# A hybrid streaming encoder step on one core: the running streams' attention in 128x32 tiles of the array

## The reference

```
k = concat([k_cache, k_new], 1); v = concat([v_cache, v_new], 1)      # 528 rows
sc = einsum('bqhd,bkhd->bhqk', q, k).astype(f32) * d**-0.5
sc = sc + rel_bias            # group A;  group B: unselected keys get -inf
p = softmax(sc); o = einsum('bhqk,bkhd->bqhd', p, v)
```

## Time and profile before

| | us |
|---|---|
| device time, median of 3 runs (2888.13 to 2890.64) | 2889.68 |
| span of the profiled execution | 2886.9 |
| TensorE busy: matmuls / weight loads | 2714.9 (94%) / 2441.3 (85%) |
| VectorE / ScalarE / GpSimd busy | 1381.5 / 673.3 / 155.3 |

### The profile page before, as it was taken

One profiled execution on the slowest core, in us unless ns is written; L12 is line 12 of the kernel. 1 busy time (PEld: TensorE's weight loads), 2 busy tenths in 40 slices (PEclk: granted clock), 3 DMA queues, 4 the chain that ended last, 5 costly groups with the idle time before them and its releaser, 6 DMA issues. The chain is left out here.

```text
span 2886.9 us, 38111 instructions
## 1 busy us (share of the span) xinstructions
PE 2714.9 (94%) x15412; PEld 2441.3 (85%) x15412; DVE 1381.5 (48%) x2539; ACT 673.3 (23%) x1228; POOL 155.3 (5%) x116
## 2 busy tenths in 40 slices
PE   6999999999998999976988989989799999999998
PEld 6999999999997799975777766667799999999997
DVE  5333333333335598986777723333333333333335
ACT  4101111111022323133666532221211111111112
POOL 0000000000001021831000000000000000000000
PEclk9999999999998999998999989999899999999999
DMA  4111111111003121213000335540211111111101
GB/s 150 54 44 44 44 44 44 44 33 39 22 17 107 48 94 63 79 48 119 30 23 30 110 104 178 178 161 1 88 44 44 44 44 44 44 44 44 44 7 66
DMA packets 117273, 180.97 MB, mean 63 GB/s; under 512 B 11424, under 2 KB 75048, under 8 KB 117168
## 3 DMA queue, kind: packets, MB, share of 16 engines
q1 hardware_dynamic: 113520, 165.35, 17.3%
q0 software_dynamic: 3648, 14.16, 1.4%
HBM read 155.73 MB, written 31.11 MB: 65 GB/s over the span
## 5 line engine op out<-in xcount | busy, mean ns | idle before, releaser
L347 DVE TENSOR_TENSOR f_silu<-f_silu,f_pgu 128x384 f32<-128x384 f32 x132 | 73.2, 554 | 802.2 <-ACT f_silu L287 802.2
L185 PE MATMUL f_pgu<-r_T_hi,f_gh 128*128 128x384 f32 x1056 | 359.7, 341 | 15.8 <-DVE f_gl L331 9.6
L186 PE MATMUL f_pgu<-r_T_lo,f_gh 128*128 128x384 f32 x1056 | 358.7, 340 | 0.0
L187 PE MATMUL f_pgu<-r_T_hi,f_gl 128*128 128x384 f32 x1056 | 358.7, 340 | 0.0
L185 PE MATMUL f_pgu<-r_T_hi,f_uh 128*128 128x384 f32 x1056 | 357.9, 339 | 0.0
L186 PE MATMUL f_pgu<-r_T_lo,f_uh 128*128 128x384 f32 x1056 | 357.6, 339 | 0.0
L187 PE MATMUL f_pgu<-r_T_hi,f_ul 128*128 128x384 f32 x1056 | 357.6, 339 | 0.0
L368 DVE SCALAR_TENSOR_TENSOR r_x<-f_pyx,r_x 128x512 f32<-128x512 f32 x396 | 267.1, 689 | 181.3 <-PE f_pyx L187 178.9
L185 PE MATMUL f_pyx<-f_dh,f_h_hi 128*128 128x512 f32 x792 | 309.4, 391 | 0.3 <-DVE r_x L368 0.3
L186 PE MATMUL f_pyx<-f_dl,f_h_hi 128*128 128x512 f32 x792 | 308.8, 390 | 0.0
L187 PE MATMUL f_pyx<-f_dh,f_h_lo 128*128 128x512 f32 x792 | 308.2, 389 | 0.0
(11 more groups left out here) (228 smaller groups left out, 4533.2 us busy)
## 6 DMA issues: line engine op xcount, KB each, us to landing
f_raw_d<-in_ffn_w_down SPq DMA_DIRECT2D x22, 1024.0 KB, 4.9
f_raw_g<-in_ffn_w_gate SPq DMA_DIRECT2D x20, 1024.0 KB, 5.4
f_raw_u<-in_ffn_w_up SPq DMA_DIRECT2D x20, 1024.0 KB, 7.9
proj<-w_stage POOLq DMA_DIRECT2D x12, 1152.0 KB, 5.6
i_raw<-in_w_in SPq DMA_DIRECT2D x12, 1024.0 KB, 5.1
t_rows<-proj SPq DMA_DIRECT2D x32, 256.0 KB, 3.0
t_kc<-in_cache_a_k SPq DMA_DIRECT2D x8, 1024.0 KB, 7.5
t_vc<-in_cache_a_v SPq DMA_DIRECT2D x8, 1024.0 KB, 5.3
```

Source lines behind the costliest of these rows:

```text
L185: pe.matmul(out, a[0], b[0], start=first, stop=False)
L186: pe.matmul(out, a[0], b[1], start=False, stop=False)
L187: return pe.matmul(out, a[1], b[0], start=False, stop=last)
L347: dve.tensor_tensor(silu[:, k % 2, :], silu[:, k % 2, :], pu[k % 2][:, 0:CW], ALU.mult).then_inc(s_free, 1)
```

## The change

In the score each head pair f gets its own 128x32 weight matrix and writes its own 32 rows of the PSUM tile, rather than being one of four accumulated 128x128 products. In the values each head pair takes its 32 columns of `pT` as weights and only the 128 columns of `v` that belong to the pair, so `po` has 128 columns; the new rows become a full 128-row product over zero rows, for which `vn` and the tail of `pT` are cleared once. The scaling is 128 columns wide and the output needs one transpose. Count for one item: the score's records stay 16 (two per instruction), the values' go from 10 of 512 columns to 40 of 128, the output's transposes from 4 to 1.

```
+Q2 = 2 * DEC_S
-        vn = [smp(f"vn{i}", [DEC_S, FW], F32) for i in range(2)]
+        vn = [smp(f"vn{i}", [P, FW], F32) for i in range(2)]
-        bd = [smp(f"bd{i}", [P, 5 * P], F32) for i in range(2)]
+        bd = [smp(f"bd{i}", [P, HT, Q2], F32) for i in range(2)]
...                                    # sync, cached_values(s)
+                if s < 2:
+                    sp.wait_ge(s_zero, 6)
-                sp.dma_start(vn[s % 2][:], proj[r:r + DEC_S, ...]).then_inc(s_vc[s % 2], 16)
+                sp.dma_start(vn[s % 2][0:DEC_S, :], proj[r:r + DEC_S, ...]).then_inc(s_vc[s % 2], 16)
...                                    # gpsimd
+            for i in range(2):
+                pool.memset(vn[i][:], 0.0).then_inc(s_zero, 1)
+            pool.memset(pT[:, :, PAST:PAST + P], 0.0).then_inc(s_zero, 1)
...                                    # diag()
-            ... [list(a.ap[0]), [P + 2 * DEC_S, HT], [1, DEC_S]])
+            ... [list(a.ap[0]), [Q2, HT], [1, DEC_S]])
...                                    # vector and scalar, turn: one more wait each
+                            dve.wait_ge(s_zero, 6)
+                            act.wait_ge(s_zero, 6)
...                                    # vector, value
-                    dve.tensor_scalar(osb[:, n % 2, :], po[:], rec[:, n % 2, 0:1], None, ALU.mult)
+                    dve.tensor_scalar(osb[:, n % 2, 0:P], po[:, 0:P], rec[:, n % 2, 0:1], None, ALU.mult)
...                                    # tensor, score
-                            last = pe.matmul(out, bd[s % 2][:, f * P:(f + 1) * P], kTs[s % 2][:, f, c0:c1],
-                                             start=f == 0, stop=f == HT - 1 and x == 0)
+                            last = pe.matmul(out[f * Q2:(f + 1) * Q2, :], bd[s % 2][:, f, :], kTs[s % 2][:, f, c0:c1],
+                                             start=True, stop=x == 0)
...                                    # tensor, value
-                    for k in range(PAST // P):
-                        pe.matmul(po[:], pT[:, s % 2, k * P:(k + 1) * P], vc[s % 2][:, k, :], start=k == 0, stop=False)
-                    pe.matmul(po[:], pT[0:DEC_S, s % 2, PAST:PAST + P], vn[s % 2][:], start=False, stop=True).then_inc(s_o, 1)
+                    for k in range(PAST // P + 1):
+                        vals = vc[s % 2][:, k, :] if k < PAST // P else vn[s % 2][:]
+                        for f in range(HT):
+                            last = pe.matmul(po[f * Q2:(f + 1) * Q2, 0:P], pT[:, s % 2, k * P + f * Q2:k * P + (f + 1) * Q2],
+                                             vals[:, f * P:(f + 1) * P], start=k == 0, stop=k == PAST // P)
+                    last.then_inc(s_o, 1)
...                                    # tensor, out
-                    pe_rows(pe, ("so", s), osb[:, (NTT + s) % 2, :])
+                    out = pe_misc(pe, ("so", s))
+                    pe.transpose(out[:, 0:P], osb[:, (NTT + s) % 2, 0:P], ident[:]).then_inc(s_mf, 1)
```

More of the change, by code:

```diff
@@ L1175, in cached_values @@
                 sp.dma_start(vc[s % 2][:], caches[x][1][0, b].rearrange("(k p) h d -> p k (h d)", p=P)).then_inc(s_vc[s % 2], 16)
+                if s < 2:
+                    sp.wait_ge(s_zero, 6)
                 r = SEQ + b * DEC_S
-                sp.dma_start(vn[s % 2][:], proj[r:r + DEC_S, x * N_QKV + 2 * FW:x * N_QKV + 3 * FW]).then_inc(s_vc[s % 2], 16)
+                sp.dma_start(vn[s % 2][0:DEC_S, :], proj[r:r + DEC_S, x * N_QKV + 2 * FW:x * N_QKV + 3 * FW]).then_inc(s_vc[s % 2], 16)
             cached_keys(0)
@@ L1216, in _ @@
                     pool.wait_ge(s_zero, 3)
-                bv = bd[s % 2][:].rearrange("p (f c) -> p f c", c=5 * DEC_S * 2)
+                bv = bd[s % 2]
                 for j, (dst, src) in enumerate(((kTs[s % 2][:, :, PAST:KS], snT[:, x, 0, :, bs]),
                                                 (bv[0:HD, :, 0:DEC_S], snT[0:HD, x, 1, :, bs]),
-                                                (bv[HD:P, :, DEC_S:2 * DEC_S], snT[HD:P, x, 1, :, bs]))):
+                                                (bv[HD:P, :, DEC_S:Q2], snT[HD:P, x, 1, :, bs]))):
                     pool.tensor_copy(dst, src).then_inc(s_bd, 1)
@@ L1228, in diag @@
             a = pm[r * HD:(r + 1) * HD, 0:DEC_S]
-            return bass.AP(a.tensor, a.offset + r * DEC_S, [list(a.ap[0]), [P + 2 * DEC_S, HT], [1, DEC_S]])
+            return bass.AP(a.tensor, a.offset + r * DEC_S, [list(a.ap[0]), [Q2, HT], [1, DEC_S]])
         def dve_out(dve, key, n):
@@ L1356, in _ @@
                         dve.wait_ge(s_mf, misc[("so", s - 2)] + 1)
-                    dve.tensor_scalar(osb[:, n % 2, :], po[:], rec[:, n % 2, 0:1], None, ALU.mult).then_inc(s_os, 1)
+                    dve.tensor_scalar(osb[:, n % 2, 0:P], po[:, 0:P], rec[:, n % 2, 0:1], None, ALU.mult).then_inc(s_os, 1)
                 else:
```

## The result

The changed kernel takes 2822.78 us (median of 4, 2820.09 to 2828.02) against 2888.90 for the kernel before on the same chip: a ratio of 0.977, 95% interval 0.9756 to 0.9784, some 66 us less. Forecast were 46 us less and 2843; the range ended at 2832, so the direction was right and the size was not.

The account below looks back on a forecast made before the run. TensorE, busy 96 to 98% of each step, was taken to set the pace. Savings of 15.6 us (band steps), 20.8 (sparse steps), 6.7 (filling) and 3.4 (tail) made 46.5 us, giving 2843 us; range 2832 to 2896.

Parts of the forecast that it names:

- TensorE sets the pace, keys hidden: In the kernel before, TensorE is busy 96 to 98% of each step; keys land 3.2 us before they are needed.
- Output transposes: Four to one per item: worth 0 in a full step, behind which TensorE waits for a VectorE copy; 0.6 us in the tail.
- Changes of shape: Switches of TensorE's array shape: some 0.19 us each; four per step before, then two in band steps, six in sparse ones.
- Scores and values: Tiled products with partial overlap: scores from 3.63 to 2.1 us (3.3 in sparse steps), values from 4.58 to 2.7 us.
- A: Partial overlap, each change of tile exposing a short load of 0.09 us: steps 10.4 and 11.56, 2875 us; chance 0.16.
- B: Tiles take turns, nothing runs side by side: steps 11.4 and 12.4, 2891 us, within 0.2%; chance 0.12.
- C: Serial loads, none beside a matmul in tile shape: steps 16.4 and 17.2, slower, 2966 us; chance 0.11.
- 8.65, set by DMA: Band step length in us: TensorE needs 8.2, but keys land 8.56 after the first key transpose, plus 0.1 for the signal.
- the full overlap: Scores and values shrink to some 1.5 and 1.8 us, both step kinds set by 8.65 of DMA: some 2834 us.
- the sparse steps' 9.4: Sparse step length in us, set by TensorE: 3.4 to the scores, 3.3 scores, 2.7 values; 20.8 us saved over these steps.
- The clock (D): Waits or half-idle tiles put the stage at 1.2 GHz: steps 14.0 and 16.4, 2941 us; chance 0.09.
- Memsets and new waits: GpSimd's clears take 1.5 us against 1.25 and end before SyncE's first new-row load; the added waits cost 0.

## Why the prediction was right and wrong

**TensorE sets the pace, keys hidden.** Right: a third key buffer does nothing for the kernel before.

**Output transposes.** Right: 0 in a step, 0.5 us once against 0.6.

**Changes of shape.** Right in kind, 0.12 in place of 0.19 each; from K to the scores it was therefore 3.53 and not 3.4.

**Scores and values.** Wrong in size, and the cause of it shown. I let the two records of an instruction block the queue, so that only two tiles worked at once: 2.1 and 2.7 us. They took 0.91 and 1.2, the low ends of my bounds (0.9, 1.1): the records of a tile follow each other, but four tiles start together. The count of tiles in turn orders the cost: 4.4, 1.8, 1.2. Scores in sparse steps 1.60 against 3.3. The sentence of the Trainium skill, "TensorE: Matmul & The Clock Gate", Part 3, that loads overlap only where row groups differ, does not hold here: these tiles share all row groups and their loads are 0.03 us apart. Its other statement, that column tiles run at once, holds; with four tiles the score group is 3.63/0.91 = 4.0 times shorter. Rivals A, B and C fall with that.

**"8.65, set by DMA".** This step failed too, and it is the one that put the time outside the range: the range allowed for the full overlap, at 2834, and its lower end stood on steps of 8.65. From the trace of before I took K and V, the end of the value group ahead of it, as one moment; they are one only while the keys are there in time. SyncE issues at V. In the changed kernel (its first load behind each V):

```profile
1738.67 0.37 SPq L1176 DMA_DIRECT2D t_vc<-in_cache_a_v  x1
...
1745.33 0.37 SPq L1176 DMA_DIRECT2D t_vc<-in_cache_a_v  x1
...
1754.39 0.37 SPq L1176 DMA_DIRECT2D t_vc<-in_cache_a_v  x1
```

V is 1745.3, but TensorE waits for keys and K comes only at 1747.72. The keys issued behind 1738.67 are the ones for 1747.72 (9.05 later), those behind 1745.33 for 1754.65 (9.3 later). Some 1 us of that goes until SyncE issues the keys and 8.1 to 8.4 until they have landed, more than the 7.5 that I took, so the error is not in the landing. And V follows the K before it by a work time: 1739.55 to 1745.33, 5.8. So the next K but one is K + work + landing: two steps cost some 5.8 + 9.1 = 14.9 us (1732.90 to 1747.72 are 14.8), 7.4 each and not 8.65. Thirteen steps measured 99.2 us; 13 x 8.65 would be 112.5. Taken behind the right size of scores and values, 13 us of the 25 missing in the stage are this step's, and of the rest 6 come from the sparse steps' 9.4 and 5 from the filling (24.1 to 12.6 us, 11.5 against 6.7), 1.5 from the tail (4.9 against 3.4). The split depends on that order: with 8.2 and 9.4 us of work, as forecast, loads that allow a shorter pace would have saved 5 x 0.45, some 2 us. The kernels with the third buffer and with small loads show that the pace was the keys' lead: both fall to 5.65.

**The clock (D).** It has a grain of truth: with the waits the stage from the first scores on is at 0.93, three steps at 0.75 or 0.76. That cost some 4 us, far from the gain.

**Memsets and new waits.** Nothing of them shows; SyncE's first load of new rows goes at 1696.01, where it went at 1694.60, the same distance from the start of the stage to 0.1 us.

**What would be better.** A third key buffer and the selection products together: 2796.66 us, 3.2% below the kernel before and 26 us below the changed one. The buffer is worth 20 of it; the selection products' share, 1.9 by the steps, is too small for the times to show.

## What to carry to other kernels

Where only 32 columns of the weights are of use, give each group its own column tile and order the products so that consecutive instructions change tile: the same 40 records cost 1.2, 1.8, 3.3 or 4.4 us by their order and tile. Once an engine that hid a load gets faster, write the load's cycle from the event that issues it, not from one that happens to coincide with it, and follow it over two steps: buffers that alternate gave here a pace of half the sum of landing and work. And an operation in front of a wait for something else costs nothing as long as that wait ends later: the three output transposes stood in TensorE's order in every step, and without them the steps were the same.

## What the hardware showed beyond that

Four column tiles took f32 records of 128 columns 0.027 us apart, where one tile takes them 0.110 apart. Ten records in a row for each tile cost 3.26 us a group with the change of shape, less than the 4.3 of strict order: with one tile and with two at a time, the next tiles started when those in hand had four records to go; by what rule is open. The 16 DMA engines gave 357 GB/s at a share of 1.02 beside band steps of 5.65 us, the length that they had with a quarter of the loads.
